# Modulation vectors by multiply-and-sum on VectorE in a two-block transformer kernel on one core

## What is computed

```python
silu_c = jax.nn.silu(c)                                   # block one, 1024 numbers
mod = jnp.einsum('bd,de->be', silu_c, w_ada[l]) + b_ada[l]  # 1024 x 6144 weights
shift1, scale1, gate1, shift2, scale2, gate2 = jnp.split(mod, 6, axis=-1)
h = modulate(rms_norm(x, norm1_w[l]), shift1, scale1)
# block two, for each of its two layers, two input vectors on one weight matrix
mod = (silu_c @ w_ada[l] + b_ada[l])[:, None, :]
mod_c = (silu_cc @ w_ada[l] + b_ada[l])[None, None, :]
```

## Time and profile before

| | us |
|---|---|
| median of three runs (2725.82 to 2728.4) | 2726.88 |
| the profiled execution, its time | 2728.38 |
| its span, first to last instruction | 2726.6 |
| PE busy in the span | 2427.8 |
| DVE busy in the span | 1698.3 |
| ACT busy in the span | 1324.8 |

### The profile page before, as it was taken

One profiled execution on the slowest core, in us unless ns is written; L12 is line 12 of the kernel. 1 busy time (PEld: TensorE's weight loads), 2 busy tenths in 40 slices (PEclk: granted clock), 3 DMA queues, 4 the chain that ended last, 5 costly groups with the idle time before them and its releaser, 6 DMA issues.

```text
span 2726.6 us, 39939 instructions
## 1 busy us (share of the span) xinstructions
PE 2427.8 (89%) x15602; PEld 2081.8 (76%) x15602; DVE 1698.3 (62%) x3163; ACT 1324.8 (49%) x2082; POOL 52.9 (2%) x63
## 2 busy tenths in 40 slices
PE   4999989999989999998988878979989997797997
PEld 2877889999956666687977657779879896676997
DVE  4566569889967677764555566555555454664554
ACT  4554444555555555554544434544454444444444
POOL 1000000000000000000000000000000000000000
PEclk8999989999999999998998687989999897878999
DMA  6554545654478878865543110036545453201553
GB/s 223 172 192 156 177 152 185 216 190 145 147 246 260 260 256 264 264 210 177 186 140 126 64 39 31 22 122 190 172 139 174 152 180 98 86 1 62 166 187 127
DMA packets 138122, 433.07 MB, mean 159 GB/s; under 512 B 15376, under 2 KB 38672, under 8 KB 137680
## 3 DMA queue, kind: packets, MB, share of 16 engines
q1 hardware_dynamic: 109424, 396.93, 45.3%
q10 hardware_dynamic: 26208, 23.98, 2.8%
q0 software_dynamic: 2304, 9.60, 1.0%
HBM read 416.56 MB, written 13.89 MB: 158 GB/s over the span
## 4 chain that ended last, share of the span: by engine, by line
PE 63%; DVE 14%; issue 9%; ACT 8%; DMA 5%; POOL 1%; ACTq 0%; POOLq 0%; SPq 0%; DVEq 0%
PE bk L1583 60%; DVE SPL L1031 6%; ACT SPL L693 4%; DMA RAW<-in_ada 3%; PE bk L1589 2%; DVE R L1031 2%; ACT R L695 1%; DVE TMP L1031 1%; DMA kept<-TMP 1%; DVE R L1040 1%; DVE ST L1046 1%; POOL ST L604 1%; ACT R L693 1%; DVE R L1037 1%; DVE R L1035 1%
## 5 line engine op out<-in xcount | busy, mean ns | idle before, releaser
L1031 DVE TENSOR_TENSOR SPL<-RAW,SPL 128x1024 fp32r<-128x1024 f32 (+1 forms) x758 | 920.0, 1222 | 564.2 <-ACT SPL L693 562.1
L693 ACT ACTIVATE SPL<-RAW 128x1024 fp32r<-128x1024 f32 (+1 forms) x758 | 791.8, 1051 | 432.9 <-PE bk L1583 378.7
L1583 PE MATMUL bk<-HH,SPL 128*128 128x256 f32 x3840 | 748.6, 288 | 25.7 <-DVE R L1031 13.2
L1583 PEld LDWEIGHTS bk<-HH,SPL 128*128 128x128 f32 x3840 | 620.3, 193 | 33.1 <-DVE R L1031 14.3
L1583 PE MATMUL bk<-SPL,WHL 128*128 128x512 f32 x2328 | 578.2, 398 | 49.7 <-DVE SPL L1031 49.7
L1583 PEld LDWEIGHTS bk<-SPL,WHL 128*128 128x128 f32 x2328 | 429.8, 190 | 166.2 <-issue 81.1
L1583 PE MATMUL bk<-HL,SPL 128*128 128x256 f32 x1920 | 546.4, 285 | 0.0
L1583 PEld LDWEIGHTS bk<-HL,SPL 128*128 128x128 f32 x1920 | 372.0, 194 | 3.1 <-issue 0.7
L1583 PE MATMUL bk<-SPL,HH 128*128 128x256 f32 (+1 forms) x1664 | 319.8, 294 | 21.6 <-DVE HL L1031 12.6
L693 ACT ACTIVATE R<-bk 128x512 f32<-128x512 f32 (+5 forms) x376 | 186.6, 508 | 271.6 <-PE bk L1583 231.9
L1583 PEld LDWEIGHTS bk<-SPL,HH 128*128 128x128 f32 x1664 | 272.9, 202 | 31.8 <-issue 15.2
(11 more groups left out here) (118 smaller groups left out, 2156.3 us busy)
## 6 DMA issues: line engine op xcount, KB each, us to landing
RAW<-in_peer SPq DMA_DIRECT2D x256, 512.0 KB, 4.8
RAW<-in_ada SPq DMA_DIRECT2D x144, 512.0 KB, 5.1
RAW<-in_ffn SPq DMA_DIRECT2D x132, 512.0 KB, 4.3
RAW<-in_win SPq DMA_DIRECT2D x96, 512.0 KB, 4.7
RAW<-in_ffd SPq DMA_DIRECT2D x66, 512.0 KB, 3.7
RAW<-in_wout SPq DMA_DIRECT2D x32, 512.0 KB, 3.8
kept<-TMP ACTq DMA_DIRECT2D x90, 128.0 KB, 2.9
TMP<-kept ACTq DMA_DIRECT2D x90, 128.0 KB, 4.6
```

Of the source, the lines that this page charges most:

```text
L693: ins = e.activation(out, in_, func, bias=bias, scale=scale)
L1031: e.tensor_tensor(out, a, b, op).then_inc(*dve.up(*points))
L1583: ins = e.matmul(out, lhsT, rhs, start=start, stop=stop, skip_group_check=True)
```

## The change

It replaces the four-matmul step by one pass on DVE. The weights are laid out by output: tile b of a matrix holds 128 outputs, one for each partition, with all 1024 weights of each. The input vector lies in `TMP` as a row of 1024, broadcast to all partitions and put through Silu there. `times_c` multiplies tile and row and sums along the row, and the sum is the modulation value of that output, in the place in `MOD` where it is wanted. For the tiles of block two that serve both streams, it does so twice. These tiles are not split and take no slot of `SPL`; the steps `ada` and `adt` are gone from TensorE, ACT and PSUM. Biases are added once for a whole range of `MOD` (`biased`).

The plan moves too. Six, six and four of the first 16 tiles stand around the first norm. `fill` keeps 32 tiles of block one. Of block two's 96 tiles the 48 of layer 0 stay in the PEER loop, at one in four steps for j from 8 on and three in four after j = 90, and the 48 of layer 1 are woven into the steps after attention: 24 into output projection and context feed-forward, 24 into the other stream's feed-forward. A step `sil2` loads the two input rows of block two (1 MB when broadcast) and applies Silu, once ahead of the PEER loop and once behind layer 0's attention. `hidden_lo` moves behind the next tile's split: into `pu` and `fy`, for the tile two ahead of theirs.

```diff
-def ada_steps(m, groups):
+def ada_steps(m, blocks):
+    return [("ada", m, b) for b in blocks]
...
-    fill = ada_steps(first, range(4, 12)) + [("A2",)]
-    late = ada_steps(l0, range(12)) + [("mods", 0)] + ada_steps(l1, range(12)) + [("mods", 1)]
+    fill = ada_steps(first, range(16, 48)) + [("A2",)]
+    late = ada_steps(l0, range(16)) + [("mods", 0, "a")] + ada_steps(l0, range(16, 48))
+    last = [("sil2", 1)] + ada_steps(l1, range(48))
...
-    plan += [("pl", j) for j in range(2)] + take(4)
+    plan += [("pl", j) for j in range(2)] + [("sil2", 0)]
...
-        peer += [("pu", j - LAG)] * (j >= LAG) + take(2 if j % 8 < 2 else 1)
+        peer += [("pu", j - LAG)] * (j >= LAG) + take(j >= 6 and (j % 4 == 0 or (j > NA and j % 2 == 1)))
...
-    plan += weave(out_steps(0, 0) + pre_steps(0, 0), out_steps(0, 1) + pre_steps(0, 1) + ffn_steps(0, 1))
+    side = weave(out_steps(0, 1) + pre_steps(0, 1) + ffn_steps(0, 1), last[:25])
+    plan += weave(out_steps(0, 0) + pre_steps(0, 0), side) + [("mods", 1, "a")]
...
-    ffn = ffn_steps(0, 0)
+    ffn = weave(ffn_steps(0, 0), last[25:])
...
+            def times_c(n):
+                dve.stage = "ring"
+                row, sums = modulation(n)
+                dve.wait_ge(T.at(*row), T.at("raw", n))
+                for k, (c, total) in enumerate(sums):
+                    last = k == len(sums) - 1
+                    if not last:
+                        dve.wait_ge(T.at("spare", doubles[-1]) if doubles else None)
+                        doubles.append(n)
+                    e.tensor_tensor_reduce(out=raw(n) if last else spare[n in in_ext], in0=raw(n), in1=c, scale=1.0, scalar=0.0,
+                                           op0=ALU.mult, op1=ALU.add, accum_out=total).then_inc(*dve.up(("times" if last else "spare", n)))
...
-                hidden_lo(key)
+                if j < LAG:
+                    hidden_lo(key)
+
+            def pu(j):
+                if j + LAG < P:
+                    hidden_lo(("peer", j + LAG))
...
+            def sil2(l):
+                if l == 0:
+                    pool.wait_ge(T.at("full", ("g", 63)), T.at("kept", NA - 1), T.at("kept", NA - 2))
+                else:
+                    pool.wait_ge(T.at("out", ("dT", 0, 0)))
+                load(f"crow2_{l}", crow2, dram["rows"][5760:7808].partition_broadcast(P))
...
-        "ada": tiles(a["w_ada"][0], 512),
-        "ada2": np.stack([tiles(a["w_ada_2"][l], 512) for l in range(2)]),
+        "ada": a["w_ada"][0].T.reshape(48, P, D),
+        "ada2": np.stack([a["w_ada_2"][l].T.reshape(48, P, D) for l in range(2)]),
```

More of the change, by code:

```diff
@@ L37 @@
 _n = 0
[L38 removed]
+for _name, _w in [("ident", 128), ("iota", 128), ("cosS", 32), ("sinS", 32), ("cosL", 64), ("sinL", 64), ("half", 20)]:
     CONS[_name] = (_n, _w)
@@ L92 @@
 STAGE = {
-    "sil": "mod", "ada": "mod", "adt": "mod", "mods": "mod", "A1": "mod", "A2": "mod",
+    "sil": "mod", "sil2": "mod", "mods": "mod", "A1": "mod", "A2": "mod",
     "norm_a": "norm", "norm_b": "norm", "nT": "norm",
@@ L313 @@
     ORDER += _keys
+IS_SPLIT = [k[0] not in ("ada", "ada2") for k in ORDER]
+SPLITS = [n for n in range(len(ORDER)) if IS_SPLIT[n]]
+SPLIT_NO = {n: k for k, n in enumerate(SPLITS)}
 def program(nc, dram, out_d, xs_d, as_d, T):
@@ L677, in df_a @@
                 power(stat(144, 8, s), stat(136, 8, s), 8, "diff", l, s)
-            steps = {"sil": sil, "norm_a": norm, "norm_k": norm, "mix_in": mix_in, "AT": at_, "ln": ln, "on": on,
+            steps = {"sil": sil, "sil2": sil2, "norm_a": norm, "norm_k": norm, "mix_in": mix_in, "AT": at_, "ln": ln, "on": on,
                      "top_in": top_in, "c_in": c_in, "nT": nT, "scl": scl, "gn": gn,
@@ L718, in sil_, with sil2 @@
             def sil_():
+                e.dma_start(crow, dram["rows"][4736:5760].partition_broadcast(P)).then_inc(*T.up("d_crow", 16, [("crow_in",)]))
                 e.dma_start(cols[:, :], dram["cols"][:, :]).then_inc(*T.up("d_cols", 16, [("cols",)]))
                 e.dma_start(cons[:, :], dram["cons"][:, :]).then_inc(*T.up("d_cons", 16, [("cons",)]))
-                act.wait_ge(T.at("cols"))
-                A(sil, cols[:, 0:24], ACT.Silu, ("sil",))
-            def ada(m, g, c):
-                if c == 3:
-                    key = ("ada", m, g)
-                    M = 2 * MODS[m][1]
-                    n = rown[(m, g)]
-                    if n >= 2:
-                        act.wait_ge(T.at("full", ("adt",) + groups[n - 2]))
-                    act.wait_ge(T.at("full", key))
-                    A(row(m, g)[0:M, :], ps(*key)[0:M, :], ACT.Copy, ("row", m, g), ("out", key))
+                act.wait_ge(T.at("crow_in"))
+                A(crow, crow, ACT.Silu, ("crow",))
+            def sil2(l):
+                act.wait_ge(T.at(f"crow2_{l}"))
+                A(crow2, crow2, ACT.Silu, ("crow2", l))
             def norm_a(t):
@@ L1118, in adt @@
-            def adt(m, g):
-                key, ns = ("adt", m, g), MODS[m][1]
-                d = v2(MODS[m][3], ns)[:, :, 4 * g:4 * g + 4]
-                dve.wait_ge(T.at("full", key))
-                tt(d, ps(*key)[:, 0:4 * ns].rearrange("p (n s) -> p s n", s=ns),
-                   MODS[m][2][:, 4 * g:4 * g + 4].unsqueeze(1).to_broadcast([P, ns, 4]), ALU.add, ("out", key))
             def a1():
-                dve.wait_ge(dve.own)
+                biased(MOD[:, 0:16], col["b_ada"][:, 0:16])
@@ L1633, in tensor_program @@
             REST = {(0, 1): (0, 1, 2), (0, 0): (5, 6, 7), (1, 0): (5, 6, 7)}
-            def ada(m, g, c):
-                cs, ns = MODS[m][:2]
-                M, key = 2 * ns, ("ada", m, g)
-                n = CHUNKS[("ada", m, g, c)][0]
-                b = take(key, MODB) if c == 0 else ps(*key)
-                pe.wait_ge(T.at("cs"), T.at("hi", n), T.at("lo", n))
-                for k in range(2):
-                    x = cs[:, (2 * c + k) * M:(2 * c + k + 1) * M]
-                    for q, y in enumerate(split(n)):
-                        last = k == 1 and q == 1
-                        done = [("used", n)] + [("full", key)] * (c == 3)
-                        mm(b[0:M, :], x, y[:, k * 512:(k + 1) * 512], c == 0 and k == 0 and q == 0, c == 3 and last,
-                           *(done if last else ()))
-            def adt(m, g):
-                ns, key = MODS[m][1], ("adt", m, g)
-                M, r = 2 * ns, row(m, g)
-                b = take(key, MODB)
-                pe.wait_ge(T.at("row", m, g), T.at("cons"))
-                for n in range(4):
-                    mm(b[:, n * ns:(n + 1) * ns], r[0:M, n * P:(n + 1) * P], con["sel"][0:M, 0:ns], True, True,
-                       *((("full", key),) if n == 3 else ()))
             def nT(t, i, k):
```

128 lines of the change are left out of this document (70 added, 58 removed).

## The result

| | before | after |
|---|---|---|
| median of the comparison, us | 2726.35 | 2666.35 (four runs, 2664.01 to 2668.39) |
| ratio | | 0.978, interval 0.976 to 0.980 |
| span of the profiled execution, us | 2726.6 | 2662.3 |

The kernel is faster by 60 us (64 by the two spans). The forecast was a gain of 165 us and 2562 us; the measured time lies 26 us above the upper end of the range, 2640. The direction is right, nearly two thirds of the gain is missing.

The account below looks back on a forecast made before the run. TensorE was taken as the bound in projections, PEER loop and feed-forward, weight arrival at the start. Terms 15 + 31 + 3 + 132 − 10 − 6 = 165 us off 2728.4, median 1.5 lower, gave 2562 us; range 2515 to 2640.

Parts of the forecast that it names:

- The cost of a sum: DVE's multiply-and-sum over 1024 elements plus its short second instruction: 1.37 us, from 1.22 to 2.4.
- half pace: Rival: a sum on DVE costs 2.4 us, PEER loop gains only 105, kernel 2661 us; chance 0.12.
- Start: Up to `A1`, limited by data arriving: `A1` at 42 us instead of 57.0, gain 15 us (5 to 20).
- Entry: Entry of the PEER loop: row loads, Silu, first product at 768 against 770.7 us; gain 3 us (−4 to 4).
- The PEER loop: Its 88 products: 3.0 us each instead of 4.50, near TensorE's floor of 2.84; gain 132 us (97 to 145).
- The move of `hidden_lo`: PEER loop: frees DVE of standing 0.48 us behind ACT's rounding; without it DVE would need 3.2 us a step.
- Projections: Input projections, 57 to 310 us: 43 us off TensorE, less 12 of new waits; gain 31 us (10 to 43).
- j from 90: 1181 to 1410 us: 54 sums, 74 us, come onto DVE; loss 10 us for waits (0 to 30).
- feed-forward: 1836 to 2244 us: 64 sums, 88 us, on DVE, TensorE's work the same; loss 6 us (0 to 20).
- signs of being wrong: Sums over 2 us; TensorE awaiting low halves in loop; feed-forward step over 0.3 us longer; cold clock, 60 to 310 us.
- DVE's order binds the loop: Rival: in the PEER loop two sums delay a hidden low half; 3.5 us a step, kernel 2621 us; chance 0.19.
- Slower: Rival: sums cost more than any row shows, DVE bounds everywhere; 2800 us at 3.3 us a sum; chance 0.04.

Follow-up runs that it names:

- short sums: The changed kernel with each multiply-and-sum over the first 16 of 1024 columns only, all else kept: 2623.51 us in one run.

## Why the prediction was wrong, step by step

**The cost of a sum** was right: 1.30 us, taken at 1.37. The rival *half pace* is refuted. The Trainium skill (Vector Engine (DVE) Microarchitecture Reference, "Points that are easy to get wrong") has the scalar-tensor-tensor form with two SBUF sources that are not bf16 at half throughput; the instruction measured here bears another name in the trace, but it is float32, multiplies two SBUF sources and accumulates, and took 1225 ns for 1024 elements against 1221 of the plain form. So this trace shows no half pace for it.

**Start** was right: `A1` at 43.5 us (42 forecast), 13.6 us gained (15):

```profile
43.54 0.17 DVE L1046 SCALAR_TENSOR_TENSOR AB<-MOD,cols 128x8 f32<-128x8 f32 x1
```

**Entry** was right within 2 us (1 gained, 3 forecast). It took the path foreseen: the rows land, then Silu, then the first product.

```profile
739.60 1.91 ACT L702 ACTIVATE TMP<-TMP 128x2048 f32<-128x2048 f32 x1 [7.41 <-DMA TMP<-in_rows]
```

**The PEER loop is the step that failed.** It added up what each engine does in a step (TensorE 2.84, DVE 2.74, ACT less), took the greatest as the bound, and set 3.0 us a product. What a step cost was 3.62 us, and most of it is the sum of what DVE and ACT do *for each other in turn*, 3.41 us in a step without sums, where DVE alone is busy 2.1 and ACT 1.5. The rows for that were there. The earlier trace rows has 41.7 us of DVE waiting for ACT's rounding and 73.9 us for ACT's high half, and the prediction used the first as DVE's idle time that the move of `hidden_lo` would free, without asking whether DVE comes round to ACT again in the same step. The "two products of slack in `SPL` and `WHL`" are slack of TensorE's, and don't loosen a chain between the two engines that fill them. Skewing DVE by a tile recovers 65 us and so shows that step; it reaches 253 us where the prediction had 265. The loop is also the only stage that lies clearly outside its term's range: 82 us gained, 97 to 145 foreseen. Small slips of the working change little: over the whole loop the step before is 4.55 us (400.7/88) and not 4.50, the densest step of the projections adds up to 6.7 us for DVE and not 6.9, and the slower case's loop gains 87 us and not 84.

**The move of `hidden_lo`** was given the wrong sign for this kernel: it costs 17 us (7 in the kernel before). The sentence that it helps is true of a kernel in which the chain is cut, by 29 us; there the prediction's account of DVE comes near what happens.

**Projections** (13 instead of 31), **j from 90** (27 lost instead of 10) and **feed-forward** (20 lost instead of 6) fail by one omission: the prediction took the waits from DVE's load and never asked what `LEAD` counts. With the lead counted in split tiles, gain and losses become 41, 8 and 4. The last two measurements lie in their terms' ranges (0 to 30) and at the edge (0 to 20), so there the size was off; the projections' 13 lies in 10 to 43 too. The plan of the kernel after also starts the context stream's steps at j = 102, not 100; no run prices that.

**The signs named.** Two of the signs of being wrong came: TensorE waited for low halves in the loop (47.8 us), and a feed-forward step is longer by 20.2/43 = 0.47 us. The clock between 57 and 300 us was 0.92, against 0.95 before.

**The rivals.** *Half pace* gave 2661 us, 5 from what was measured, and that is luck: its sum of 2.4 us was measured at 1.30. *DVE's order binds the loop*, 3.5 us a step and 2621 us, is nearest in the loop's step (3.62), and was right that order and not load decides. Its mechanism was another, though: the pair of sums ahead of a hidden low half. The chain closes in steps that have no sums at all, and short sums bring 25 us where the skew brings 65. Its chance of 0.19 was too low, and the range ended at 2640 because the lead was in no case. Either cure alone brings the kernel into the range (2633.53 and 2593.33 us). *Slower* and *doesn't do what it says* played no part.

**What stays open.** The 4 us from product 171 on need no cause in the change: the kernel before with the skew in its loop has the kernel before's steps there and took 441.5 us too. The loop's 65 us over the skewed kernel are 45 of idle time of TensorE and 21 of busy time at the lower clock. The two come together in these runs, and none separates them; since the chain of DVE and ACT sets the pace, it isn't shown that the slower matmuls cost anything by themselves.

## What to carry to other kernels

Adding up each engine's work in a step gives a lower bound only; walk once round the loop through every engine that waits for another, and if the walk comes back to its start within the step, its length is the step. Work taken from the busiest engine uncovers such a chain, and the cure may be a skew of one tile in one engine's list (65 us here) and not less work. When a kind of tile leaves one engine, look at everything that counts tiles (here a lead of two, worth 73 us). And read what a moved instruction waits for in the order it will have: the same move was worth +29 us in one kernel and −17 in another.

## What the runs showed of the hardware

The multiply-and-sum on DVE costs 1.22 us for 1024 float32 columns plus 0.08 us for storing the sum; I had bounded that second part by ACT's like instruction, 0.19. A TensorE that pauses every few products (busy 270 of 319 us) was granted a mean clock of 0.92 over the loop, with eleven short stretches at 1.2 GHz, and took 250 ns a matmul (270.17/1081), against 230 ns (248.91/1081) at 0.99 in the kernel that hardly pauses (249 of 253 us): the same matmuls, 21 us more.
